# Slot table of a mixture of experts: one-hot products on VectorE and TensorE, or indirect transfers into memory

## What is computed

```python
g_idx = jnp.argmax(g_logits, axis=-1)
e_sel = jnp.take_along_axis(e_logits, g_idx[:, None, None], axis=1)[:, 0]
top_v, top_i = lax.top_k(e_sel, TOP_K)
top_w = jax.nn.softmax(top_v, axis=-1) * g_p
expert_id = g_idx[:, None] * EXPERTS_PER_GROUP + top_i
...
for e in range(N_EXPERTS):
    h = jax.nn.silu(xt @ w_gate[e]) * (xt @ w_up[e])
    y = y + gate[:, e:e + 1] * (h @ w_down[e])
```

## Time and profile before

| | |
|---|---|
| runs | 904.5, 905.51, 907.43 us; median 905.51 |
| the profiled execution's own time | 906.62 us |
| its span, first to last instruction | 904.8 us |
| mean granted clock of TensorE | 0.955 |
| busy: TensorE, VectorE, ScalarE, POOL | 823.6, 587.5, 441.7, 266.9 us |
| tiles of experts that ran (copies L964) | 26 |
| HBM read and written | 144.79 and 28.24 MB |

### The profile page before, as it was taken

The page is one execution under the profiler, slowest core; times in us unless marked ns, Lnnn a source line. Parts: engine busy times, 40 slices in busy tenths (PEclk is TensorE's granted clock), DMA queues, the critical chain, the costliest instruction groups (busy, mean ns, idle before and its releaser), DMA issues.

```text
span 904.8 us, 12786 instructions
## 1 busy us (share of the span) xinstructions
PE 823.6 (91%) x4275; PEld 716.4 (79%) x4276; DVE 587.5 (65%) x732; ACT 441.7 (49%) x494; POOL 266.9 (29%) x259
## 2 busy tenths in 40 slices
PE   5999999999999999279999999999999999999900
PEld 5999999998788886168888888888888888888800
DVE  4079999966675564879988983148811624937148
ACT  5122232436733223428898883258732725846233
POOL 3333465472000000024343432124321413323225
PEclk9999999999999999569999999999999999999965
DMA  8211111103547331568999999149962663983174
GB/s 287 54 47 41 39 38 46 46 24 113 209 171 284 133 112 58 152 237 282 392 391 371 394 394 315 28 113 366 382 198 62 198 187 85 359 270 87 25 233 173
DMA packets 59407, 167.34 MB, mean 185 GB/s; under 512 B 6757, under 2 KB 25190, under 8 KB 55286
## 3 DMA queue, kind: packets, MB, share of 16 engines
q1 hardware_dynamic: 51318, 144.57, 42.9%
q0 software_dynamic: 8064, 22.45, 11.7%
HBM read 144.79 MB, written 28.24 MB: 191 GB/s over the span
## 4 chain that ended last, share of the span: by engine, by line
PE 88%; DVE 6%; DMA 3%; ACT 1%; issue 1%; SPq 0%; POOL 0%; ACTq 0%; POOLq 0%; DVEq 0%
PE PS L1541 32%; PE PS L1315 21%; PE PS L1557 16%; PE PS L1471 10%; PE PS L1294 5%; DVE C L1074 1%; PE PS L1442 1%; DMA MIX<-in_x_prompt 1%; PE PS L1359 1%; DVE RAW L1271 1%; PE PS L1423 1%; DVE BIG L384 1%; DMA sum_rows<-F,MIX 1%; DMA F<-x_rows,MIX 1%; DMA RAW<-sum_rows 0%
## 5 line engine op out<-in xcount | busy, mean ns | idle before, releaser
L1541 PE MATMUL PS<-BIG,TH 128*128 128x512 f32 x1248 | 297.3, 395 | 1.5 <-DVE TH L1230 1.5
L1541 PEld LDWEIGHTS PS<-BIG,TH 128*128 128x128 f32 x1248 | 234.7, 190 | 49.7 <-issue 1.9
L1315 PE MATMUL PS<-BIG,WD 128*128 128x352 f32 x1152 | 190.9, 327 | 2.5 <-DVE BIG L1003 2.5
L1315 PEld LDWEIGHTS PS<-BIG,WD 128*128 128x128 f32 x1152 | 188.0, 190 | 3.6 <-DVE BIG L1003 2.7
L325 DVE TENSOR_TENSOR BIG<-RAW,BIG 128x2048 fp32r<-128x2048 f32 x64 | 145.1, 2288 | 24.4 <-ACT BIG L900 24.4
L1557 PE MATMUL PS<-WD,TH 128*128 128x512 f32 x624 | 156.1, 400 | 0.0
L1557 PEld LDWEIGHTS PS<-WD,TH 128*128 128x128 f32 x624 | 113.6, 189 | 22.1
L900 ACT ACTIVATE BIG<-RAW 128x2048 fp32r<-128x2048 f32 x64 | 119.0, 1908 | 15.5 <-PE PS L1471 7.9
L292 DVE SCALAR_TENSOR_TENSOR PS<-RAW,C,PS 128x512 f32<-128x512 f32 x174 | 115.3, 747 | 0.0
L1471 PE MATMUL PS<-BIG,WD 128*128 128x512 f32 (+1 forms) x432 | 100.7, 392 | 1.7 <-DVE BIG L384 1.7
L1471 PEld LDWEIGHTS PS<-BIG,WD 128*128 128x128 f32 (+1 forms) x432 | 76.8, 179 | 22.6 <-issue 1.3
(11 more groups left out here) (201 smaller groups left out, 767.2 us busy)
## 6 DMA issues: line engine op xcount, KB each, us to landing
RAW<-in_w_gate SPq DMA_DIRECT2D x64, 512.0 KB, 7.4
RAW<-in_w_up SPq DMA_DIRECT2D x64, 512.0 KB, 9.1
MIX<-in_w_down SPq DMA_DIRECT2D x32, 1024.0 KB, 10.4
F<-in_w_in SPq DMA_DIRECT2D x17, 512.0 KB, 4.1
F<-in_x_prompt SPq DMA_DIRECT2D x10, 512.0 KB, 4.7
x_rows<-F SPq DMA_DIRECT2D x9, 512.0 KB, 2.7
sum_rows<-F SPq DMA_DIRECT2D x9, 512.0 KB, 3.6
RAW<-in_w_out SPq DMA_DIRECT2D x4, 1024.0 KB, 6.2
```

The costliest lines, as they stand in the source:

```text
L1315: mm = pe.matmul(bank(3 * q + g, GRP), win[:, q, ws, c, :], xT[:, xs_, c, g * GRP:(g + 1) * GRP], start=(c == 0 and ws + xs_ == 0), stop=( ...
L1541: mm = pe.matmul(bank(h), xe[:, xs_, c, :], w, start=(c == 0 and xs_ + ws == 0), stop=(c == KD - 1 and xs_ == 1))
```

## The change

The table of rows is no longer made by products for all tiles.

- *Tiles 0 and 1* get their row numbers by comparison. For tile 0, `key0` is the rank where expert 0 is the first of the tile's experts (and a number out of range elsewhere); one comparison of 128 x 1152 on VectorE (`places`), 9 matmuls of two columns, a copy and a sum give `idx01[0]`. For tile 1 the two choices' slot numbers are compared, with 18 matmuls of two columns, to `idx01[1]`. The first two gathers take these directly, without copy and addition.
- *All others, and all gates:* a table in memory, `tab_dram`, with 64 bytes for each slot. POOL fills it ahead of time with blanks. When the slot numbers are ready, POOL enters row number and gate of each choice by 18 indirect transfers, one for each token tile and choice, with the second gather behind the sixth. SP, behind the loads of expert 1, waits for all 18 and reads the first 8 bytes of each of the 4480 entries back into `tabs`, of which `table` and `gates` are now views. ScalarE's first scaled copy and POOL's `index(2)` wait for this (`table_in`).
- The six gate operations move ahead of the wait for the ranks; `lo_unit(0, 2)` moves behind the remainder of tile 0.

The diff, cut to its core:

```diff
+    tab_dram = nc.dram_tensor("slot_rows", (NTAB * P, 16), F32).ap()
...
+        pay = mx(2 * NT * 16).rearrange("p (k i w) -> p k i w", k=2, i=NT)
+        tabs = mx(2 * NTAB)
+        tabv = tabs.rearrange("p (t w) -> p w t", w=2)
+        table, gates = tabv.bitcast(U32)[:, 0], tabv[:, 1]
...
             load_expert(1)
+            sp.wait_ge(S("rows_entered"), 16 * 2 * NT)
+            sp.dma_start(tabs.rearrange("p (t w) -> p t w", w=2),
+                         tab_dram.rearrange("(t p) w -> p t w", p=P)[:, :, 0:2]).then_inc(S("table_in"), 16)
...
+            pool.dma_start(tab_dram.rearrange("(t p) w -> p t w", p=P)[:, :, 0:2],
+                           tabs.rearrange("p (t w) -> p t w", w=2)).then_inc(S("table_blank"), 16)
...
-            pool.wait_ge(S("table_ready"), 1)
-            index(0)
+            def gather(t):
+                pool.wait_ge(S("index_copied"), t - 1)
+                pool.tensor_tensor(carrier[:, 0:1], epsc, epsc, ALU.add)
+                gather_rows(idxc)
+
             pool.wait_ge(S("x1_stored"), 16 * NT)
-            gather(0)
-            pool.wait_ge(S("rows_in"), 16)
-            index(1)
-            pool.wait_ge(S("xe_turned"), 1)
-            gather(1)
+            pool.wait_ge(S("first_index"), 1)
+            gather_rows(idx01[0])
+            pool.wait_ge(S("table_blank"), 16)
+            pool.wait_ge(S("slots_ready"), 1)
+            pool.wait_ge(S("payload_ready"), 2)
+            for n in range(2 * NT):
+                c, i = n // NT, n % NT
+                M = rows_of(i)
+                if n == 6:
+                    pool.wait_ge(S("first_index"), 2)
+                    pool.wait_ge(S("xe_turned"), 1)
+                    gather_rows(idx01[1])
+                pool.indirect_dma_start(tab_dram, bass.IndirectOffsetOnAxis(ap=slot[0:M, c, i:i + 1], axis=0),
+                                        pay[0:M, c, i, :], None).then_inc(S("rows_entered"), 16)
             pool.wait_ge(S("rows_in"), 32)
+            pool.wait_ge(S("table_in"), 16)
             index(2)
...
-                act.wait_ge(S("gates_ready"), 1)
+                act.wait_ge(S("table_in"), 16)
...
+            do(dve.scalar_tensor_tensor(key0, Mb[:, :, 0], -float(FAR), rk[:, :, 0], ALU.mult, ALU.add))
+            do(dve.tensor_scalar(vc0[:, :, 1], key0, -1.0, pm, ALU.mult, ALU.add))
+            places(ohf[:, 0], ig, key0).then_inc(S("first_hot"), 1)
...
+            first_index(0)
...
+            dve.tensor_copy(slot, slf).then_inc(S("slots_ready"), 1)
+            do(dve.tensor_scalar(vc1[:, :, :, 1], slf, -1.0, p128, ALU.mult, ALU.add))
             for c in range(2):
...
+                places(ohf[:, 1 + c], ig1, slf[:, c]).then_inc(S("first_hot"), 1)
             lo_unit(dve, 0, 1)
-            lo_unit(dve, 0, 2)
+            first_index(1)
...
-            for u in (3, 4, 5):
+            for u in (2, 3, 4, 5):
                 lo_unit(dve, 0, u)
...
+            pe.wait_ge(S("first_hot"), 1)
+            first_rows(0, vc0, 0, True, True).then_inc(S("first_sum"), 1)
+            pe.wait_ge(S("first_hot"), 3)
+            pe.wait_ge(S("first_index"), 1)
+            first_rows(1, vc1[:, 0], 2, True, False)
+            first_rows(2, vc1[:, 1], 2, False, True).then_inc(S("first_sum"), 1)
```

More of the change, by code:

```diff
@@ L203, in build @@
         ntf, inc, exc, ci, ci2 = (mx(NE) for _ in range(5))
[L204 to L217, removed]
+        slf = mx(2 * NT).rearrange("p (k i) -> p k i", k=2)
+        wgt = [pay[:, k, :, 1] for k in range(2)]
+        ohf = RAW[:, OFF_BC:OFF_BC + 3 * NT * P // 2].bitcast(BF16).rearrange("p (k i m) -> p k i m", k=3, i=NT)
+        tabf = mx(4)
         idxc = mx(1).bitcast(U32)
-        otw = mx(3 * NT * NTAB).bitcast(BF16).rearrange("p (k i h m) -> p k i h m", k=2, i=NT, h=3)
-        gatep = mx(3 * NTAB)
-        gates = mx(NTAB)
+        idx01 = [mx(1).bitcast(U32) for _ in range(2)]
         padc = mx(1)
@@ L1232, in _ @@
             ins.then_inc(S("xe_lo"), 1)
-            dve.wait_ge(S("gate_sum"), 1)
-            do(dve.tensor_copy(gatep, bank(7, 3 * NTAB)))
-            do(dve.tensor_tensor(gates, gatep[:, 2 * NTAB:], gatep[:, NTAB:2 * NTAB], ALU.add))
-            dve.tensor_tensor(gates, gates, gatep[:, 0:NTAB], ALU.add).then_inc(S("gates_ready"), 1)
-            for u in (3, 4, 5):
+            for u in (2, 3, 4, 5):
                 lo_unit(dve, 0, u)
@@ L1496, in _, with first_rows @@
             mm.then_inc(S("ranked"), 1)
-            for c in range(2):
-                pe.wait_ge(S("one_hot"), c + 1)
+            def first_rows(c, values, col, start, stop):
                 for i in range(NT):
                     M = rows_of(i)
-                    mm = pe.matmul(bank(6, 2 * NTAB), ohp[0:M, c, i], oht[0:M, c, i].rearrange("p h m -> p (h m)"),
-                                   start=(c + i == 0), stop=(c == 1 and i == NT - 1))
-            mm.then_inc(S("table_sum"), 1)
+                    mm = pe.matmul(bank(5)[:, col:col + 2], ohf[0:M, c, i], values[0:M, i],
+                                   start=(start and i == 0), stop=(stop and i == NT - 1))
+                return mm
+            pe.wait_ge(S("first_hot"), 1)
[4 more added lines that the diff above has]
+            first_rows(2, vc1[:, 1], 2, False, True).then_inc(S("first_sum"), 1)
             def turn_xe(t):
@@ L1515, in turn_hid @@
                 mm.then_inc(S("hid_turned"), 1)
-            for c in range(2):
-                for i in range(NT):
-                    M = rows_of(i)
-                    if c + i == 0:
-                        pe.wait_ge(S("gate_hot"), 3)
-                    mm = pe.matmul(bank(7, 3 * NTAB), ohp[0:M, c, i], otw[0:M, c, i].rearrange("p h m -> p (h m)"),
-                                   start=(c + i == 0), stop=(c == 1 and i == NT - 1))
-            mm.then_inc(S("gate_sum"), 1)
             pe.wait_ge(S("rows_in"), 16)
```

88 lines of the change are left out of this document (38 added, 50 removed).

## The result

The changed kernel takes **919.16 us**, the median of 4 runs (918.52 to 919.61); the kernel before, on the same chip, 906.47 (904.5 to 907.89). The ratio is 1.0143, with a 95% interval from 1.0128 to 1.0158: slower, and above the upper end of the predicted range. The span of the profiled execution grew from 904.8 to 917.9 us.

A forecast was written before the change was run, and what follows sets the result against it. The path from ranks through row numbers and first gather to tile 0 was taken to bound the end. Terms -6.9 + 0.7 + 1.3 = -4.9 us from the median 905.5 gave 900.6; range of 8 in 10: 898 to 913.

The forecast's parts named there:

- Tile 0: Start of the first tile on TensorE: earlier row numbers and gather bring it to 387.2 us, 6.9 us earlier.
- An entry takes 1.07 us: POOL's 18 indirect transfers: each costs 1.07 us, as a gather does, so the last starts at 399.1.
- the right mechanism as a rival: On POOL: VectorE's two-SBUF-operand subtractions shut entries out, last entry about 415, table in at 422.5, time 914; chance 0.22.
- The rival of dear entries: On POOL: each entry costs 1.65 us like the accumulating scatter, table in at 416.5, time 906.7; chance 0.17.
- Landing: After the last entry's start: its data takes 6.8 us to land, beside expert 1's weight loads, at 405.9.
- the read: SP's read of 4480 pieces of 8 bytes from the table: about 4.5 us, table in at 410.4.
- Slack of 1.3 us behind ScalarE's copy: From ScalarE's first scaled copy to TensorE's transposes: a table up to 409.7 costs nothing, each later microsecond one; here 0.7.
- A microsecond saved is a microsecond of the end: Between the ranks and tile 0: time saved there shortens the whole kernel equally, as long as nothing later turns late.

The follow-up runs named there:

- p1: Changed kernel, with VectorE's low-part weight subtractions (all but the first) taking their second operand from PSUM instead of SBUF; 907.25 us.
- its control: Kernel before, with the same edit of VectorE's subtraction (second operand from PSUM) and no entries; 910.45 us.
- h3: Kernel before with tile 0's row numbers by comparison, no entries; gate sums behind a branch in the tile loop, added up before unit 5's low part; 905.38 us.
- h1: Kernel before with tile 0's row numbers by comparison, no entries, tile 0 written out ahead of the loop, GpSimd taking low parts of units 4 and 5; 919.22 us.
- h2: Same as h1, but the low parts of units 4 and 5 left to VectorE behind the gate products; 911.2 us.

## Why the prediction was wrong

**Tile 0, right.** Forecast 387.2, measured 386.90. The rows landed at 383.33 (forecast 382.9), and the 18 matmuls ended at 383.50 (383.7). Within this, the gather started 0.9 us later than forecast and took 0.5 us less to land.

**An entry takes 1.07 us: here it failed.** The value was read from the gathers, 1.04 to 1.35 us, and none of those 28 begins while a subtraction L325 runs, since the addition ahead of each takes that wait; the 18 entries run beside nine. Alone an entry takes 0.97 and starts every 1.27 us (p1); here every 1.9. The last entry was 15.9 us late: 11 or so are the holding, 3.6 come of the 0.30 us between two starts, which the sum had at nothing (0.97 + 0.30 against 1.07, 18 times), and 0.9 of a later first entry. The prediction had the right mechanism as a rival, with the last entry at about 415 (measured 415.03), the table in at 422.5 (421.34) and a second fall of the clock, and gave it 0.22. It weighed against it that L690 was not held; but L690 had begun 0.4 us ahead of the subtraction, as the entry at 385.95 did. What is ahead of a subtraction is not held, so that row was no evidence, and L662, begun in the middle of one, was. (The rival of dear entries cites the same copy for the scatter's 1.65 us; it ended with the subtraction and says nothing of the scatter, whose own row has the 1.65.)

**That rival's price, 914, was too low.** It had 12.8 us for the wait in tile 1 (11.2), up to 3.2 for the clock (3.7), and 1.3 for the third gather (5.1). From table to gather POOL took 5.6 us instead of 4.0, and the gather, itself held (2.95), landed in 10.65 us instead of 6.8. Two smaller terms stood in no sum, and nearly cancel: 1.72 us of waiting for tile 1's rows, and 1.2 us less at half the clock in tile 0 (42 matmuls in 11.51 us instead of 12.71).

**Landing, too long; the read, right.** The table was to be in 6.8 + 4.5 us after the last entry; it was 6.3 us. The read was 4.34 us (4.5); the last entry, with SP's loads held back, landed in 1.95 instead of 6.8. In p1 the table was in at 409.5, close to the forecast 410.4, by luck: there the entries took 4 us longer than forecast and the landing 5 less.

**Slack of 1.3 us behind ScalarE's copy, right.** From copy to transposes 9.10 us before (415.33 to 424.43), 7.83 now (421.52 to 429.35).

**"A microsecond saved is a microsecond of the end": only in part.** Free of the block, the change gives 3.2 us against its control, not 4.9, and the early first tile alone 0.7, which is not to be told from nothing. Between 470 and 560 us the weight loads leave TensorE little room to come earlier: 2 us of h3's lead go there. The prediction looked at the DMA share around the routing alone.

## What to carry to other kernels

Before work goes to GpSimd's queue, look at what VectorE does in the same stretch, and count its operations with two SBUF operands: an indirect transfer that starts while one runs lasts until that one has ended, and a short operation of VectorE with two SBUF inputs can wait for long ones of GpSimd just so. Price a table by the time at which its last part arrives, at each of its readers: with two readers of one table, freeing the first only uncovered the second. And before a lead is booked to the end, look for the next stage whose DMA share is already 1.

## What was not expected of the hardware

- GpSimd holds VectorE up as VectorE holds GpSimd: 9.83 us (h1) for a subtraction that alone takes 0.18 (h2). The Trainium skill, SBUF — State Buffer, Who interferes with whom, has it that issue order decides who blocks. The entries agree: those that start while a subtraction runs are held, that at 385.95, ahead of one, is not. The row of h1 does not, as it is recorded: VectorE's subtraction starts at 394.29, 0.74 us ahead of GpSimd's first, and is the one that is held; why is open.
- An entry of 128 times 64 bytes landed 2.1 us after its start where the DMA share was under 0.1 (405.54), and 5.9 where the weight loads had it at 1.04 (396.74), while POOL was free again after 0.97 in both cases.
- The start of a loop behind a tile written out ahead of it cost TensorE 4.4 us with nothing to wait for (h2), and 1.8 where it begins ahead of tile 0 (h3). What fills this time was not looked into.
